# First-half convolution moved off TensorE, chunk slots and pool weight buffers reshaped, norm rows requested earlier, a table of unit priorities

## The reference, cut to what matters

```python
h = rms_norm(x, norm_mix_pre)
x_lru, g_lru, x_pool, gates = split(h @ w_in)            # 1024, 1024, 512, 2048 columns
x_lru = causal_depthwise_conv(x_lru, conv_w, conv_b)     # width 4, own weights per channel
r, i = sigmoid(x_lru @ w_a + b_a), sigmoid(x_lru @ w_x + b_x)   # 16 blocks of 64x64
a = exp(-8 * r * softplus(-lam)); u = sqrt(1 - a*a) * i * x_lru
y_lru = scan(h_t = a_t * h_{t-1} + u_t) * gelu(g_lru)
y_pool = ((trailing mean over 2, 4, 8 or 16 tokens - token) @ pool_w) * pool_scale
m = (sigmoid(gate_a) * (y_lru @ w_lru_up) + sigmoid(gate_b) * (y_pool @ w_pool_up)) @ w_o
x = x + rms_norm(m, norm_mix_post)
f = square(relu(rms_norm(x, norm_mlp_pre) @ w_ff1)) @ w_ff2     # 1024 -> 4096 -> 1024
out = x + rms_norm(f, norm_mlp_post)
```

## Time and profile before

| | us |
|---|---|
| runs (median; lowest; highest) | 925.36; 923.02; 926.18 |
| the profiled execution, its own time | 928.2 |
| its span, slowest core (6) | 926.5 |
| its span, fastest core (5) | 915.1 |
| TensorE busy, core 6 | 899.0 (97%) |
| VectorE busy | 482.2 (52%) |
| ScalarE busy | 380.3 (41%) |
| GpSimd busy | 138.7 (15%) |

### The profile page before, as it was taken

How to read it: one execution, slowest core, us unless ns; L and a number is a source line. 1 busy time by engine, 2 the same in 40 slices (tenths; PEclk the granted TensorE clock), 3 DMA queues, 4 the chain that set the end, 5 groups by cost and what they waited for, 6 DMA issues and landing times.

```text
span 926.5 us, 13471 instructions; the slowest of 8 cores (915.1 to 926.5 us)
## 1 busy us (share of the span) xinstructions
PE 899.0 (97%) x4268; PEld 408.5 (44%) x4268; DVE 482.2 (52%) x716; ACT 380.3 (41%) x590; POOL 138.7 (15%) x259
## 2 busy tenths in 40 slices
PE   6998899999999999899999999999999999999997
PEld 2443344443444444344444444444444444444443
DVE  5976867867768665666576443222123334312122
ACT  5774976465554755333455433111012333301001
POOL 2330222211122113222112111000001111000000
PEclk9999999999999999999999999999999999999999
DMA  8964787897779665666388995321224544211221
GB/s 223 201 122 91 99 106 93 111 116 117 101 108 146 100 113 122 197 141 166 81 212 241 204 219 90 46 81 57 91 87 96 79 74 76 46 46 58 80 92 45
DMA packets 46726, 105.97 MB, mean 114 GB/s; under 512 B 5313, under 2 KB 8129, under 8 KB 46402
## 3 DMA queue, kind: packets, MB, share of 16 engines
q0 software_dynamic: 27504, 53.10, 40.7%
q1 hardware_dynamic: 18864, 51.91, 17.7%
q10 hardware_dynamic: 290, 0.11, 0.1%
HBM read 141.41 MB, written 25.17 MB: 180 GB/s over the span
## 4 chain that ended last, share of the span: by engine, by line
PE 86%; DMA 5%; issue 4%; ACT 2%; DVE 2%; SPq 0%; POOL 0%; DVEq 0%; ACTq 0%; POOLq 0%
PE pp L484 85%; ACT big L460 2%; DMA big<-wpool 2%; DMA big<-x 2%; DMA big<-gains 1%; PE pp L599 1%; DVE big L468 1%; DVE big L790 0%; SPq L501 0%; DVE big L473 0%; ACT L460 0%; POOL st L586 0%; DVE big L614 0%; DVE big L716 0%; DVE big L538 0%
## 5 line engine op out<-in xcount | busy, mean ns | idle before, releaser
L484 PE MATMUL pp<-big 128*128 128x512 bf16 x3984 | 874.8, 381 | 10.7 <-ACT big L460 2.6
L484 PEld LDWEIGHTS pp<-big 128*128 128x128 bf16 x3984 | 389.1, 98 | 484.5 <-issue 38.1
L460 ACT ACTIVATE big<-pp 128x512 f32<-128x512 f32 (+3 forms) x239 | 160.1, 677 | 412.2 <-PE pp L484 391.9
L468 DVE SCALAR_TENSOR_TENSOR big<-pp,big 128x512 bf16<-128x512 f32 x128 | 88.0, 690 | 125.7 <-ACT big L460 116.0
L473 DVE TENSOR_TENSOR big<-pp,big 128x512 f32<-128x512 f32 (+1 forms) x48 | 41.5, 866 | 169.1 <-ACT big L460 156.0
L460 ACT ACTIVATE big<-pp,dv 128x512 f32<-128x512 f32 x128 | 83.2, 687 | 81.7 <-PE pp L484 73.1
L460 ACT ACTIVATE big<-big 128x1024 f32<-128x1024 f32 (+1 forms) x64 | 66.7, 1055 | 31.4 <-DVE big L473 20.8
L501 POOL DMA_DIRECT2D big<-wff x64 | 34.9, 545 | 283.2 <-PE pp L484 273.6
L468 DVE SCALAR_TENSOR_TENSOR big<-big,st 128x1024 bf16<-128x1024 f32 (+1 forms) x64 | 63.2, 1011 | 6.0 <-POOL st L588 5.0
L468 DVE SCALAR_TENSOR_TENSOR big<-big 128x512 f32<-128x512 f32 (+2 forms) x72 | 51.7, 743 | 21.8 <-ACT big L460 21.6
L468 DVE SCALAR_TENSOR_TENSOR big<-big,pp 128x512 bf16<-128x512 f32 (+1 forms) x64 | 43.5, 682 | 35.0 <-PE pp L484 21.3
(11 more groups left out here) (61 smaller groups left out, 213.7 us busy)
## 6 DMA issues: line engine op xcount, KB each, us to landing
big<-x SPq DMA_DIRECT2D x32, 512.0 KB, 6.8
big<-wff POOLq DMA_DIRECT2D x64, 256.0 KB, 4.0
w2b<-wff POOLq DMA_DIRECT2D x16, 512.0 KB, 8.4
big<-wmrga POOLq DMA_DIRECT2D x32, 256.0 KB, 6.3
x1s<-big SPq DMA_DIRECT2D x16, 512.0 KB, 5.4
big<-w2b SPq DMA_DIRECT2D x32, 256.0 KB, 5.4
big<-x1s SPq DMA_DIRECT2D x16, 512.0 KB, 3.8
out<-big SPq DMA_DIRECT2D x32, 256.0 KB, 2.1
```

The source lines that it names most:

```text
L460: return e.activation(out=o, in_=i, func=func, scale=scale, bias=bias, **kw)
L468: return add("dve", lambda e: e.scalar_tensor_tensor(out=val(out), in0=val(in0), scalar=scalar, in1=val(in1), op0=op0, op1=op1), reads, wr ...
L484: ins = e.matmul(bank(t, 512, half), lhsT=l, rhs=r, start=(i == 0), stop=(i == len(ls) - 1))
```

## The change

1. The half-0 branch of the convolution is gone; both halves go one way. After each quarter's projection ScalarE reads the PSUM bank twice: a copy to `xl` in bf16, and an `Identity` with the last tap as scale and the bias as bias, which writes the start of the sum into the slot's I buffer. Then VectorE adds the other three taps over 1024 tokens, and casts. `convd` and `conv_diag` go.
2. The slots: A and I four times, M twice; the scan writes into I; the input gate's tanh goes to small buffers of its own (`tnh`).
3. `ringP` has two buffers.
4. In the start: the norm row is asked for ahead of the identity, `setup_dv` waits for the fourth norm factor of the first half, six warmup matmuls instead of ten behind `gain_rows`, and the fifth x load waits until the fourth has landed.
5. `gains[1]` and `gains[2]` are asked for after the second and the fifth `D1_unit` of half 0.
6. The casts of `w_ff2`: four follow `D2_unit` 4 to 7 of half 0, eight the `D1_unit`s of half 0, four `D2_unit` 0 to 3 of half 1.
7. `D2_unit` of half 0 counts its banks under a kind of its own (Z). The second half's first x loads wait for the first pool projection in place of the last x load.
8. `P.rank(PRIO)` replaces every `vt` by a number of a table: all operations of one stage, one old `vt`, one engine and one kind (transfer or not) are a unit, and there is one number for each unit.

```diff
+PRIO = [float(v) for v in (
+    "43.8 51.6 -10.7 36.0 -7.4 44.1 -12.1 -3.0 -2.7 -8.4 -10.7 -24.9 -65.1 6.1 37.5 14.6 37.1 5.2 -31.3 30.0 -7.5 "
...
+).split()]
-    BANKS = {"X": 2, "C": 2, "R": 2, "G": 2, "P": 2, "D": 4, "T": 2, "E": 3, "F": 4, "Y": 3, "L": 2}
+    BANKS = {"X": 2, "C": 2, "R": 2, "G": 2, "P": 2, "D": 4, "Z": 4, "T": 2, "E": 3, "F": 4, "Y": 3, "L": 2}
+    def rank(self, prio):
+        units = {}
+        for o in self.ops:
+            k = (o["stage"], o["vt"], o["eng"], o["dma"] is not None)
+            o["vt"] = prio[units.setdefault(k, len(units))]
...
-    slotA = [R(O_AIM + 12 * s, 4, F32) for s in range(3)]
-    slotI = [R(O_AIM + 12 * s + 4, 4, F32) for s in range(3)]
-    slotM = [R(O_AIM + 12 * s + 8, 4, F32) for s in range(3)]
+    slotA = [R(O_AIM + o, 4, F32) for o in (0, 8, 12, 20)]
+    slotI = [R(O_AIM + o, 4, F32) for o in (4, 32, 16, 24)]
+    slotM = [R(0, 4, F32), R(O_AIM + 28, 4, F32)]
+    tnh = [R(4 + 2 * s, 2, F32) for s in range(2)]
...
-    ringP = R(O_RP, 2, BF16, "p (k n) -> p k n", n=128)
+    ringP = [R(o, 2, BF16, "p (k n) -> p k n", n=128) for o in (O_RP, O_XCB)]
...
+    ld("act", grow.ap[0:1, :], GAINS[0:1, :], grow.k(), "g0", 4096, -22.0)
     ld("act", identf.ap, IDENT, identf.k(), "ident", 65536, -20.0)
...
-    pre_w = warmup(10, -26.0, [gain_rows()], 3.0)
+    pre_w = warmup(6, -26.0, [gain_rows()], 2.0)
...
-                add("dve", lambda e, xl=xl, o0=o0, tx=tx: e.tensor_copy(out=xl.flat[:, o0:o0 + 512], in_=bank(tx)),
-                    [], xl.k(o0, o0 + 512), vt=vt, ps=[tx], cost=cV(512))
...
-                tc = P.tile("C")
-                mm([tc], [(tc, 0, [convd.ap[:, c * 4 + k4, :] for k4 in range(4)],
-                           [xl.flat[:, qq * 512 + k4:qq * 512 + k4 + 512] for k4 in range(4)])],
-                   convd.k(c * 512, c * 512 + 512) + xl.k(qq * 512, qq * 512 + 515), vt)
...
+                act(xl.flat[:, 3 + lo:3 + hi], lambda tx=tx: bank(tx), AF.Copy, [], xl.k(3 + lo, 3 + hi), vt, ps=[tx])
+                act(xc.ap[:, lo:hi], lambda tx=tx: bank(tx), AF.Identity, [("cvt",)], xc.k(lo, hi), vt, ps=[tx],
+                    scale=cvt[:, C_CW + c * 4 + 3:C_CW + c * 4 + 4], bias=cvt[:, C_CONVB + c:C_CONVB + c + 1], ptr=2)
...
+            for k4 in range(3):
+                stt(xc.ap, xl.flat[:, k4:k4 + 1024], cvt[:, C_CW + c * 4 + k4:C_CW + c * 4 + k4 + 1], xc.ap, ALU.mult,
+                    ALU.add, [("cvt",)] + xl.k(k4, k4 + 1024) + xc.k(), xc.k(), vt0, n=1024)
+            add("dve", lambda e, xc=xc, xb=xb: e.tensor_copy(out=xb.ap, in_=xc.ap), xc.k(), xb.k(), vt=vt0, cost=0.62)
...
-        a_, b_, c_ = A_tile(i, xinA0[i], "xa%d" % i, -10.0 + 0.5 * i, "act" if i in (5, 7) else "dve", (),
+        a_, b_, c_ = A_tile(i, xinA0[i], "xa%d" % i, -10.0 + 0.5 * i, "act" if i in (5, 7) else "dve", xl[3:4] if i == 4 else (),
                         hbA0[i], [pre_w])
...
+    setup(rso[3:4])
...
+        d2.append(D2_unit(0, j, (48 + 12.0 * j, 54 + 12.0 * j), [xl[7]]))
+        if j >= 4:
+            cast_w2(j - 4, d2[-1], 60.0 + 12.0 * j)
...
-    ld("sp", gains[1].ap, GAINS[1:2, :].partition_broadcast(128), gains[1].k(), "g1", 300000, 150.0, hard=state["gelu"][-1:])
-    ld("sp", gains[2].ap, GAINS[2:3, :].partition_broadcast(128), gains[2].k(), "g2", 300000, 151.0, hard=state["gelu"][-1:])
     for j in range(8):
         i = D1_unit(0, j, (142 + 10.0 * j, 147 + 10.0 * j))
-        cast_w2(8 + j, i, 150.0 + 10.0 * j)
+        cast_w2(4 + j, i, 150.0 + 10.0 * j)
+        if j in (1, 4):
+            n = 1 + j // 4
+            ld("sp", gains[n].ap, GAINS[n:n + 1, :].partition_broadcast(128), gains[n].k(), "g%d" % n, 1 << 20, 150.0, hard=[i])
...
     for j in range(8):
-        D2_unit(1, j, (225 + 10.0 * j, 230 + 10.0 * j))
+        i = D2_unit(1, j, (225 + 10.0 * j, 230 + 10.0 * j))
+        if j < 4:
+            cast_w2(12 + j, i, 235.0 + 10.0 * j)
...
+    P.rank(PRIO)
     P.emit(final_wait=["o0_0", "o0_1", "o1_0", "o1_1"])
```

More of the change, by code:

```diff
@@ L113, in choose_banks @@
             kinds = {}
+            nfree = sum(1 for b in range(8) if bank_tile[b] is None)
             for t in o["opens"]:
@@ L529, in fn @@
             return ins
-        i = add("pe", fn, ones.k() + grow.k(), [], vt=-27.0, ps=[t], cost=2.0)
+        i = add("pe", fn, ones.k() + grow.k(), [], vt=-27.0, ps=[t], cost=3.6)
         add("dve", lambda e: e.tensor_copy(out=gains[0].ap, in_=psum[t.bank // 2][:]), [], gains[0].k(), vt=-27.0, ps=[t],
@@ L557, in setup_dv, with setup @@
                                scalar2=None, op0=ALU.mult)
-    add("dve", setup_dv, [("cvt",)], [("dv",)], vt=2.0, cost=1.4)
+    def setup(after):
+        add("dve", setup_dv, [("cvt",)], [("dv",)], vt=2.0, cost=0.9, after=after)
     def softplus(after):
@@ L704, in B_group @@
-                add("dve", lambda e, xl=xl, o0=o0, tx=tx: e.tensor_copy(out=xl.flat[:, o0:o0 + 512], in_=bank(tx)),
-                    [], xl.k(o0, o0 + 512), vt=vt, ps=[tx], cost=cV(512))
-                if h == 0 and qq == 1:
-                    add("dve", lambda e, xl=xl, c=c: e.tensor_copy(out=halo[:, c * 4:c * 4 + 3],
-                                                                   in_=xl.flat[:, 1024:1027]),
-                        xl.k(1024, 1027), [("halo", c)], vt=vt, cost=0.07)
@@ L719, in B_group @@
-                add("dve", lambda e, xc=xc, xb=xb: e.tensor_copy(out=xb.ap, in_=xc.ap), xc.k(), xb.k(), vt=vt,
-                    cost=0.38)
-                gates(c, xb.ap, xb.k(), xc.ap, xc.k(), qq * 512, qq * 512 + 512, vt)
+                lo, hi = qq * 512, qq * 512 + 512
+                act(xl.flat[:, 3 + lo:3 + hi], lambda tx=tx: bank(tx), AF.Copy, [], xl.k(3 + lo, 3 + hi), vt, ps=[tx])
+                act(xc.ap[:, lo:hi], lambda tx=tx: bank(tx), AF.Identity, [("cvt",)], xc.k(lo, hi), vt, ps=[tx],
+                    scale=cvt[:, C_CW + c * 4 + 3:C_CW + c * 4 + 4], bias=cvt[:, C_CONVB + c:C_CONVB + c + 1], ptr=2)
@@ L722, in B_group @@
+            for qq in range(2):
+                lo, hi = qq * 512, qq * 512 + 512
+                gates(c, xb.ap[:, lo:hi], xb.k(lo, hi), lo, hi, vt0)
         vtb = vts[2]
@@ L779, in P_group @@
             t = P.tile("P")
-            mm([t], [(t, 0, [ringP.ap[:, k, :] for k in range(8)], hsl(q))], ringP.k() + hq(q), vt)
+            mi = mm([t], [(t, 0, [rp.ap[:, k, :] for k in range(8)], hsl(q))], rp.k() + hq(q), vt)
             o0 = 16 + qq * 512
@@ L978, in build_nc @@
         rso.append(b_)
+    setup(rso[3:4])
     softplus(rso[-1:])
-    for c in range(1, 8):
-        conv_diag(c, [rso[3 if c == 1 else 7]])
     gate_maps([xl[3]], [xl[6]])
```

80 lines of the change are left out of this document (30 added, 50 removed), and 51 rows, old and new, of the table PRIO.

## The result

The changed kernel takes 909.5 us (median of 4 runs, 908.65 to 910.06), the kernel before 925.3 us in the same session (923.02 to 926.18). The ratio is 0.9832, with the 95% interval 0.9812 to 0.9852: 15.8 us faster, where 18.3 (925.36 to 907) were forecast. The range of 893 to 920 holds it. Some executions, of most kernels here, had one die at a lower clock and took several per cent longer; the ratios leave them out and the medians don't, so differences between kernels are read from the ratios.

The account below looks back on a forecast made before the run. TensorE bounds the kernel, busy 97% of the span. Terms -13.8 + 3 - 2.5 - 3.9 - 4.0 + 3 = -18.2 against the profiled 928.2 us give 910.0, or 907 us by the median; range 893 to 920.

Parts of the forecast that it names:

- the forecast: Whole kernel: 907 us, with 902 to 913 as its own range, given 43%.
- Convolution matmuls (-13.8): Convolution on TensorE: 64 matmuls fewer at 0.216 us where it is the busy engine, 13.8 us less.
- rival 2: Half 0 takes as long as now: TensorE's 13.8 us turn into idle, ScalarE needs 139 us again; 918 us, 20%.
- Half 0's cover (+3): Half 0, three nearly equal engine loads: ScalarE's new work partly shows, 3 us lost; bounds -8 and +20.5.
- Start (-2.5): Start: with `setup_dv` moved back, norm row copy and all after come earlier, 2.5 us gained; bounds -4 and +1.
- Pool weight (-3.9): Half 1's second pool load: two buffers remove 2.24 us of wait and 1.7 of clock loss; bounds -3.9 and 0.
- norm rows (-4.0): First output tiles: norm rows asked for some 150 us earlier can't be late, 4.0 us gained; bounds -5.4 and 0.
- Moved casts and the new order (+3): Queues reshuffled by the table, four casts moved to half 1's merge: late weights cost 3 us; bounds 0 and 12.
- What would show it: Signs: first projection about 20 us, no `wpool` or `gains` wait, clock 0.994 or more, ScalarE 412, VectorE 477, half 0 earlier.

Follow-up runs that it names:

- experiment 2: Changed kernel, same order, with four overwritten matmuls ahead of each half-0 recurrent-input projection (64 put back): 919.32 us, ratio 0.9921 to the kernel before.
- experiment 1: Changed kernel with the hand-written due values instead of the table, all other edits kept: 923.96 us, ratio 0.9991 to the kernel before.
- experiment 3: Changed kernel, same order, without half 0's 16 `Identity` passes on ScalarE (last tap and bias missing): 907.43 us, ratio 0.9800 to the kernel before.
- experiment 7: Changed kernel with the start's tiles in natural order and column vectors asked for first, fifth x load still held: 907.54 us, ratio 0.9809 to the kernel before.
- experiments 7 and 8: Changed kernel with the start's tiles in natural order, with and without the hold of the fifth x load: ratios 0.9809 and 0.9856 to the kernel before.
- experiments 10 and 11: Kernel before, own order, with only the norm rows asked for early, and with only a second pool buffer in half 1: 924.66 and 924.22 us.
- experiment 5: Changed kernel without the table and without half 0's 16 `Identity` passes (last tap and bias missing): 924.05 us, ratio 0.9986 to the kernel before.
- experiment 9: Changed kernel, same order and loads, with more warmup matmuls in the start (12 for 6, 18 for 3): 910.25 us, ratio 0.9828 to the kernel before.
- experiment 10: Kernel before, other orders frozen, with only the two norm rows asked for early: 924.66 us, ratio 0.9997 to the kernel before.

## Why the prediction was right, and where it wasn't

The time is 2.5 us from the forecast, and the mechanism of the largest term holds. Several of the other terms don't, and that their errors cancel is luck: too much was expected of the convolution's matmuls, of the start and of the two late loads, and too little of the order.

*Convolution matmuls (-13.8): right, on a condition that I didn't see.* In the changed kernel they are worth 8 to 9.5 us (experiment 2), and the mark at the end of half 0 comes 13.5 us earlier; in the hand-written order all seven edits together, this one among them, are worth nothing (experiment 1). The 43% for the forecast and the 20% for rival 2 were bets on one question, which the profile of before could not answer: whether the order holds three engines at 84 to 91% at the same time.

*Half 0's cover (+3): right in sign, 2 us too large, and for another reason.* From the first projection to the mark TensorE is idle for 8.5 us after and 8.1 before (25.70 to 142.34 and 22.68 to 155.98 us). Over the 0.216 us of a 512-column matmul at the full clock, 460 of them now take 6.2 us more (105.62 - 460 x 0.2162) and 538 took 5.5 more (121.79 - 538 x 0.2162), so 0.7 us go to the clock. Together +1.1. I gave ScalarE's work as the cause, but 12.5 us less of it bring 1 to 3 us (experiment 3). The price of the `Identity` was too low, 0.781 us where 0.687 was taken, 3 us over the kernel; that cost nothing either:

```profile
L525 ACT ACTIVATE big<-pp,cvt 128x512 f32<-128x512 f32 x32 | 25.0, 781 | 1.5
```

*Start (-2.5): wrong sign.* The first projection is 3.0 us later. Some transposes are done ahead of it that came behind it before (seven tiles in place of five), so the loss is less: what is left of the 13.6 us from mark to mark is 16.8 (78 x 0.216) - 1.1 - 13.6 = 2.1 us, and 2.1 come back when the tiles go in their natural order (experiment 7). The step that failed is "With the setup moved back the copy can start at about 9.4 and all that follows comes up to 2.6 us earlier": it looked at one instruction ahead of the norms, and not at the table, by which TensorE's second set of transposes needs a tile that is ready late (3.67 us of wait). The edits of the start by themselves do what it says: the copy starts at 8.11 us, 12.01 before, and in experiment 1, which has them without the table, the first projection comes at 18.6 to 19.8 us on the eight cores, 3 us earlier than before. Core 3 of it:

```profile
19.84 1.89 PE L549 MATMUL pp<-big 128*128 128x512 bf16 x8 [1.16 <-DVE big L671]
```

The table then costs more than the edits bring. The identity's cast, too, now waits for its load on VectorE ahead of the first norm (core 4 of the changed kernel):

```profile
11.10 0.23 DVE L572 CAST big<-big 128x128 bf16<-128x128 f32 x1 [1.77 <-DMA big<-ident]
...
11.37 1.28 DVE L533 SCALAR_TENSOR_TENSOR big<-big,st 128x1024 bf16<-128x1024 f32 x1
```

The hold, which I counted as a loss ("VectorE then has gaps"), is a gain of 4.3 us in the order of experiments 7 and 8, by what the planner makes of it.

*Pool weight (-3.9) and norm rows (-4.0): right as a sum against the execution that was read, but not two terms, and too large for the kernel.* Both waits are gone, and behind half 0 core 4 after is 9.4 us better than core 6 before (271.3 - 264.9 + 3.0); the two prices with their clock were 9.3. In the mean over the cores it is 6.5, and with the choice of the execution taken out some 4, for all that lies behind half 0. I took the prices from the slowest core of one execution, which had both waits: the same piece is 267.7 us in the mean and 262.4 on core 5. And each edit alone brings under 1 us, in the mean core as in the slowest (experiments 10 and 11), where 3.9 and 4.0 were written. The step that failed is the addition of two prices, each as if nothing else changed: with the norm rows moved, six of eight cores wait longer for the pool weight than any did before; with the pool weight moved, the wait for the norm rows is still there. How much the two bring together no run shows, and experiment 1, which has neither wait, doesn't have the gain.

*Moved casts and the new order (+3): wrong sign, and the largest number of all.* The casts cost no wait: in 280 to 310 us the DMA share is 1.04 as before, and TensorE is full at clock 1.00. The order is what the result hangs on: 14.5 us (923.96 - 909.5; 14.7 by the ratios), and all of it is in what is planned for the first 150 us. The sum had it as a cost only. It decides whether the gain of the edits comes, and is larger than the convolution's term (8 to 9.5 us, experiment 2). What the table would bring without the other edits was not run, so the 14.5 us are its worth beside them.

*What would show it:* no wait for `wpool` or `gains`, VectorE's and ScalarE's busy times and the earlier end of half 0 came as said; the first projection and the clock (0.989 to 0.996 for 0.994 or more) didn't. The idle time from 65 to 110 us is 7.2 us on core 4, where about 10 was forecast and 7.95 was there before. The clock is lost between 85 and 100 us. There TensorE had a wait of 2.65 us and then, within 5 us, four more of 0.86, 0.22, 0.23 and 0.58. The kernel before is idle for as long in 80 to 100 us (5.6 us, 4.9 after), in waits of at most 1.3 us, and keeps the full clock (core 4 after, then core 6 before):

```profile
85.00:90.00 5.00, 1.78 (x10) 0.67 (x10) 5.00 (x7) 4.89 (x8) 3.56 (x2) 0.78 0.10 9
90.00:95.00 5.00, 4.21 (x13) 1.46 (x14) 5.00 (x10) 4.92 (x8) 2.46 (x2) 0.50 0.46 90
95.00:100.00 5.00, 5.00 (x22) 2.21 (x20) 2.89 (x5) 4.16 (x5) 0.76 (x3) 0.70 0.15 58
```

```profile
80.00:100.00 20.00, 14.43 (x61) 5.57 (x60) 13.90 (x31) 12.57 (x17) 2.70 (x5) 1.00 0.29 43
```

The Trainium skill, TensorE: Matmul & The Clock Gate, has two sections on this: HAM oscillation, which the prediction weighed, asks for longer idle stretches, and that of the second HAM failure mode says that small idles between groups of matmuls, coming often, bring the clock down too. The traces agree with the second: in 55 to 110 us the clock is 0.91 with the table, 0.84 in experiment 1 and 0.81 in experiment 5 (cores 4, 3 and 3), with 8.5, 12.5 and 11.1 us idle and no wait over 2.65 us that ends in it. The kernel before shows that idle time alone doesn't say it: 7.95 us of it in the same stretch, at 1.00.

*What stays open:* which feature of the table's order in half 0 makes the difference. The runs show only that it isn't the amount of work on ScalarE, and that it is decided in the first 150 us. Open too are the table without the other edits, and the two load edits together without the rest.

## What to carry to other kernels

Before an edit that moves work from the busiest engine to others, ask whether the order lets three engines overlap at 85 to 90%; if each now waits its turn at 75%, the time saved turns into idle, and the order is to be changed in the same step. Read the price of a wait on all cores: in one execution of the kernel before it was 0 to 2.4 us for the pool weight and 0.5 to 4.5 for the norm rows. Don't add the prices of two late loads: here moving one made the other later. And where a planner orders the work, compare the sequences before giving a moved load the credit: here holding one load back changed what stands ahead of the first projection, and the first tiles landed no sooner.

## What the runs showed of the hardware

The granted clock's column doesn't tell the rate in the start. The windows view of core 4 has 1.00 for 8 to 16 us:

```profile
8.00:16.00 8.00, 4.97 (x18) 1.79 (x17) 6.12 (x10) 5.61 (x12) 3.31 (x6) 1.00 0.99 268
```

But there the six warmup matmuls of 512 columns take 2.74 us together, and twelve take 5.30 us in experiment 9 (core 3), so 0.43 us from one to the next (2.56 / 6), twice the 0.216 of the earlier trace rows, which is the lower of the two levels; and eight transposes take 1.01 us at 12.80 and 0.61 at 137 us. So the start is to be read from durations. Twenty-one more warmups didn't change the time (experiment 9).

A load of 256 KB on GpSimd's queue took 18.8 us to land (core 1 of experiment 10) when norm rows, broadcast to 128 partitions, went out on SP's queue 5 us ahead of it; the median of the 64 `wff` loads of the same size is 4.4 us in the changed kernel, that of the 32 `wmrga` loads 9.5:

```profile
big<-wff POOLq DMA_DIRECT2D x64, 256.0 KB, 4.4
...
big<-wmrga POOLq DMA_DIRECT2D x32, 256.0 KB, 9.5
```
